# Two blocks of a sequence model in one launch: the order of VectorE's work in an attention step, and of one low part on GpSimd

## The reference

```
# 16 heads of 64, 4 key/value heads, blocks of 128 queries against 256 keys
s = einsum('bnqkgd,bnjkd->bnkgqj', qb, kk) * (HEAD_DIM ** -0.5)
s = where(mask, s, NEG_INF)
m = maximum(max(s, axis=-1), sink)
pr = exp(s - m)
w = pr / (sum(pr, axis=-1) + exp(sink - m))
o = einsum('bnkgqj,bnjkd->bnqkgd', w, vv)
h = h + o @ w_o
hm = h * rsqrt(mean(h * h) + eps) * norm_mlp      # rmsnorm, then the MLP
```

## Time and profile before

| | |
|---|---|
| time, median of 3 runs | 1812.46 us (1812.0 to 1815.38) |
| the profiled execution's own time | 1810.39 us |
| its span, first to last instruction | 1808.6 us |
| PE busy | 1744.2 us, 96% of the span |
| DVE, ACT, POOL busy | 898.0, 767.4 and 982.2 us |
| mean granted TensorE clock | 0.986 |
| attention loop | about 1243 to 1375 us |
| `wob` and the first two units of `up1` | about 1375 to 1412 us |

### The profile page before, as it was taken

One profiled execution on the slowest core, in us unless ns is written; L12 is line 12 of the kernel. 1 busy time (PEld: TensorE's weight loads), 2 busy tenths in 40 slices (PEclk: granted clock), 3 DMA queues, 4 the chain that ended last, 5 costly groups with the idle time before them and its releaser, 6 DMA issues.

```text
span 1808.6 us, 20962 instructions
## 1 busy us (share of the span) xinstructions
PE 1744.2 (96%) x8022; PEld 1424.6 (79%) x8022; DVE 898.0 (50%) x1298; ACT 767.4 (42%) x1205; POOL 982.2 (54%) x616
## 2 busy tenths in 40 slices
PE   9999999999997779999999999999999999999998
PEld 7887888777786777888888888887567788888886
DVE  3999987676674774532212122656655221212124
ACT  5333335377755573344223323533555331323234
POOL 5859555676555573654444445665436444444464
PEclk9999999999998999999999999999999999999999
DMA  4223223222221223223222223232102222322321
GB/s 166 98 90 100 100 92 125 86 88 81 100 79 49 65 84 132 97 94 101 93 96 103 93 95 103 83 105 70 36 24 70 93 93 96 102 94 94 104 93 59
DMA packets 54532, 164.05 MB, mean 91 GB/s; under 512 B 6304, under 2 KB 14112, under 8 KB 54304
## 3 DMA queue, kind: packets, MB, share of 16 engines
q1 hardware_dynamic: 54432, 162.71, 26.8%
HBM read 156.66 MB, written 6.03 MB: 90 GB/s over the span
## 4 chain that ended last, share of the span: by engine, by line
PE 65%; DVE 6%; ACT 5%; issue 4%; POOL 3%; DMA 0%; SPq 0%; POOLq 0%; DVEq 0%; ACTq 0%
PE B L313 52%; PE B L2226 1%; PE B L2137 1%; PE B L1634 1%; POOL ACC L366 1%; ACT WH L285 1%; PE B L296 1%; PE B L298 1%; PE B L297 1%; POOL WL L289 1%; PE B L1527 1%; DVE SW L1131 1%; PE B L2208 1%; PE B L1399 0%; PE B L2335 0%
## 5 line engine op out<-in xcount | busy, mean ns | idle before, releaser
L289 POOL TENSOR_TENSOR WL<-RAW,WH 128x1024 fp32r<-128x1024 f32 x281 | 682.5, 2431 | 623.6 <-ACT WH L285 623.5
L285 ACT ACTIVATE WH<-RAW 128x1024 fp32r<-128x1024 f32 x281 | 296.5, 1057 | 664.3 <-PE B L313 631.8
L313 PE MATMUL B<-P0h,WH 128*128 128x512 f32 x1104 | 434.1, 393 | 1.8 <-ACT WH L285 1.8
L313 PE MATMUL B<-P0l,WH 128*128 128x512 f32 x1104 | 426.4, 391 | 1.4 <-DVE P0l L430 1.3
L313 PE MATMUL B<-P0h,WL 128*128 128x512 f32 x1104 | 279.8, 391 | 1.9 <-POOL WL L289 1.9
L313 PEld LDWEIGHTS B<-P0h,WH 128*128 128x128 f32 x1104 | 208.4, 189 | 47.0 <-issue 2.9
L313 PEld LDWEIGHTS B<-P0l,WH 128*128 128x128 f32 x1104 | 208.3, 189 | 46.0 <-DVE P0l L430 2.3
L313 PEld LDWEIGHTS B<-P0h,WL 128*128 128x128 f32 x1104 | 207.9, 188 | 45.6 <-POOL WL L289 2.3
L437 DVE TENSOR_TENSOR H<-H,B 128x512 f32<-128x512 f32 x88 | 60.2, 685 | 281.1 <-PE B L313 281.1
L313 PE MATMUL B<-P1h,WH 128*128 128x512 f32 x448 | 174.7, 390 | 0.0
L1907 DVE SCALAR_TENSOR_TENSOR TMP<-B,RS 128x512 f32<-128x512 f32 x64 | 44.1, 691 | 260.1 <-PE B L313 244.0
(11 more groups left out here) (354 smaller groups left out, 2797.7 us busy)
## 6 DMA issues: line engine op xcount, KB each, us to landing
RAW<-in_w SPq DMA_DIRECT2D x281, 512.0 KB, 3.2
H<-in_xT SPq DMA_DIRECT2D x8, 256.0 KB, 5.1
g<-GB SPq DMA_DIRECT2D x8, 256.0 KB, 2.2
GB<-g SPq DMA_DIRECT2D x32, 64.0 KB, 2.0
out<-Q SPq DMA_DIRECT2D x4, 512.0 KB, 3.6
u<-TMP SPq DMA_DIRECT2D x7, 256.0 KB, 2.0
U<-u SPq DMA_DIRECT2D x28, 64.0 KB, 2.0
SPT<-in_ssm SPq DMA_DIRECT2D x1, 1040.0 KB, 5.7
```

The lines of the kernel that those rows point to most:

```text
L285: act.activation(WH[:, i % NS, :], RAW[:, i % NR, :], ACT.Copy).then_inc(*inc("w_hi", i))
L289: pool.tensor_tensor(WL[:, i % NS, :], RAW[:, i % NR, :], WH[:, i % NS, :].bitcast(F32), ALU.subtract).then_inc(*inc("w_lo", i))
L313: return pe.matmul(b[:, :], w[:, ws[c]], x[:, c, :], start=start, stop=stop)
```

## The change

DVE's list in a step of the attention loop is put in another order. Before: mask (n, 0), maximum (n, 0), sum and reciprocal of n-1, mask (n, 1), maximum (n, 1), the three small ones, then rope and `woa` work, then the low part of output n-2. After: sum and reciprocal of n-1, the low part of output n-3 (so the one that stood at the end of the step before), both masks, both maxima, the three small ones, then rope and `woa` work. The last output's low part follows behind the loop. On POOL, the low part of the weights that stood between the additions of squares 6 and 7 now stands behind that of square 7.

```
     def dve_scores(dve, n, hp):
         kv, blk, k0, nk, p_ = place(n)
-        st = AS[:, n, :]
         sv = s_view(n, hp)
...
         dve.scalar_tensor_tensor(sv, bv, 0.125, mv, ALU.mult, ALU.add).then_inc(*inc("att_s", ("s", n, hp)))
-        dve.wait_ge(*at("att_s", ("s", n, hp)))
-        dve.tensor_reduce(st[:, 2 * hp:2 * hp + 2], sv, AX.X, ALU.max).then_inc(*inc("att_d", (n, "max", hp)))
-        if hp == 0:
-            return
+
+    def dve_maxima(dve, n):
+        kv = place(n)[0]
+        st = AS[:, n, :]
+        for hp in range(2):
+            dve.wait_ge(*at("att_s", ("s", n, hp)))
+            dve.tensor_reduce(st[:, 2 * hp:2 * hp + 2], s_view(n, hp), AX.X, ALU.max).then_inc(
+                *inc("att_d", (n, "max", hp)))
         sk = sink[:, 4 * kv:4 * kv + 4]
...
         for n in range(18):
+            if 0 < n < 17:
+                dve_sum(dve, n - 1)
+            if n > 2:
+                dve_out(dve, n - 3)
             if n < 16:
                 dve_scores(dve, n, 0)
-            if 0 < n < 17:
-                dve_sum(dve, n - 1)
-            if n < 16:
                 dve_scores(dve, n, 1)
+                dve_maxima(dve, n)
...
-            if n > 1:
-                dve_out(dve, n - 2)
             if n == 2:
                 dve_p(dve, 1)
+        dve_out(dve, 15)
         dve_wo(dve, "woa", 7)
...
         for n in range(8):
             add_square(pool, "mlp1", n)
-            if n % 2 == 0:
+            if n in (0, 2, 4, 7):
                 lows(pool, IDX[("wob", 0, n // 2)] + 4)
```

## The result

The change takes 1803.74 us (median of 4 runs, 1802.59 to 1805.32) against 1812.23 us for the kernel before (4 runs, 1810.19 to 1815.38): a ratio of 0.9946, with a 95% interval of 0.993 to 0.9961. It is faster, by 8.5 us where 5.1 were forecast; the forecast time was 1807.4 us. A later series of the same pair gave 0.9956 (0.994 to 0.9971). The two profiled executions are 7.0 us apart, 1810.39 and 1803.37 us.

A forecast was written before the change was run, and what follows sets the result against it. PE is busy nearly all the time, its loop idle nearly all waits on DVE's mask; 2.05 us in the loop plus 3.05 behind it, 5.1 us, gives 1807.4 us from 1812.46. Bounds 1801.0 to 1818.4, range 1803.0 to 1811.2.

The forecast's parts named there:

- The squares: Behind the loop, POOL's edit: PE's 1.40 us wait for the last square and the 1.65 us low clock go, 3.05 us.
- The order, gain: In the attention loop, DVE's edit: second mask 1.0 us earlier against the first, 2.05 us gained in the loop.
- step 3's two waits turned into one: PE's first wait grows from 0.71 to about 1.6 us, the second of 0.89 goes, low clock kept: 0 gained.
- steps 6, 7 and 16 without a wait: PE's waits in these steps of the loop go: 0.3, 1.06 and 0.4 us gained.
- The order, price: POOL's low part starts earlier and can lie over DVE's small operations: 1.1 us held in step 3, some 1.5 in step 10.
- the small account of tenths: In steps 5 and 14 the last small operation just passes ahead of POOL's low part, by 0.1 us.
- one of the prediction's own signs of being wrong: In the profile after, L2167 or L2169 lasting over 2 us in steps 5, 7 or 14 would be wrong.
- the rule for two SBUF inputs: A two-SBUF-input VectorE instruction and a GpSimd one reading SBUF exclude each other; up to 2.3 us loss per low-part step.
- The first step: Step 11 of the loop: one wait of about 1.35 us in place of 1.67, 0.3 us gained, low clock kept.
- The rival that had this in it: More of the loop comes back, in step 11 or as low clocks: up to 3.3 us more, about 1804.2 us; 22%.
- The second: Base of the sum: profiled execution 2.07 us below the median, so 5.1 us is taken from the median, 1812.46.
- The slower rival: POOL's low part holds DVE in every loop step that has one: 5.7 us lost plus 3.3 low clock, 1818.4 us; 6%.

The follow-up runs named there:

- e1_square: The kernel before with only POOL's low part moved behind square 7, DVE's order kept; 1813.9 us, ratio 0.9977 to before.
- e3_maxima_between: The change with each maximum put back behind its own mask; 1808.94 us, ratio 0.9954 to before.
- e5_exp_waits_neg: The kernel before with the four exponentials waiting for the negated maxima alone, no longer for the last small operation; 1810.44 us, ratio 0.9966 to before.
- e2_order: The change with only DVE's new order, POOL's low part ahead of square 7 as before; 1805.91 us, ratio 0.994 to before.
- e6_low_halves: The change with each of the attention's low parts on POOL split into two instructions of 512 columns; 1801.72 us, ratio 0.9914 to before.
- e4_sum_behind_masks: The change with sum and reciprocal behind both masks, ahead of the maxima; 1814.25 us, ratio 0.9984 to before.

## Why the prediction was right and where it failed

**The squares** were right in every step: the order on GpSimd, the room on TensorE, the half clock that goes with the wait. 3.05 us forecast, 3.25 us in the tails of the two profiles; every kernel with this edit has a tail of 12.06 us, those without it 15.3.

**The order, gain.** Right: the masks 0.6 us apart, the first mask in its place, no wait left at the output product, step 3's two waits turned into one (1.56 us, I had 1.6), steps 6, 7 and 16 without a wait. In step 6 this was luck: the 0.3 us were to come because the hold of 2.29 us in step 5 was to go, and it stayed, at 2.27 us. Idle time in the loop was to fall by 2.05 us and fell by 4.99 - 3.11 = 1.88.

**The order, price.** That the low part would hold small operations was right, the small account of tenths was not, and one of the prediction's own signs of being wrong came up: a small operation of over 2 us in steps 5 and 7. Step 3 (1.29 us) and step 10 (1.65 us) were held as forecast. Step 5 was to pass by 0.1 us and was held for 2.27 us, which cost nothing more than before, since 2.29 us stood there already. Step 7 I had taken as free; the low part started 0.02 us ahead of the small operation and made the wait of 0.55 us in step 8. Step 14 passed. Step 11 came out at 1.00 us for 1.35. The errors nearly cancel: 0.55 us more in step 8, 0.35 less in step 11. And the 2.29 us with which the prediction says that the trace agrees with the rule for two SBUF inputs belong to L2169, which has one; L2170, which has two, shows it, with 2.40 to 2.45 us in e1_square.

**Two steps failed.** The forecast was 3.6 us too slow. Of these, 1.9 lie between the two profiled executions (7.0 us for 5.1), nearly all of it the 1.7 us of the first step below, and 1.7 in the way from profile to median, the second.

The first step is a term of the sum: "one wait of about 1.35 in place of 1.67: 0.3, low clock kept". The wait of 1.00 us in step 11 brought no half clock in any of the three profiles of this order, which is 1.7 us more. Why it doesn't stays open, for the length of the wait doesn't decide it: the two waits in step 11 of e3_maxima_between sum to 1.60 us and brought none, the two of before sum to 1.67 and brought one in all three profiles. The rival that had this in it named 1804.2 us and got 22%; of the 3.0 to 3.3 us that it adds, the profiles show these 1.7, so that the measured time lies so near its own is in part chance.

The second is the base of the sum: "it stands 2.07 below the median of the runs, so against the median I forecast". The distance was carried over from before to after without asking what it was, and it doesn't carry over: the profiled execution of the change lies 0.37 us below its median. Nor was "before, that low part mostly starts just behind the small operations" a fact of the kernel with one outcome. It is a race with a margin of 0.03 to 0.04 us, lost in a part of the executions; a lost one holds the chain for some 2.4 us and cost TensorE between nothing (steps 3 and 7 of e1_square) and 2.3 us of waits (step 10).

How much of the 8.5 us of the medians is the race's stays open. The two profiles account for 7.0 of them, and with four runs on each side the interval (7.1 to 12.7 us) begins there. For the race in the remaining 1.5 us speak e5_exp_waits_neg, which was to take only its price away and gains 6.0 us by the medians with a profile that gains 0.2, and e2_order, with 8.5 to 13.3 us by its ratio for 3.8 by a loop that is held against races won. Against it stands that the loop starts up to 4.2 us apart in executions of these kernels, for what happens ahead of it: the third profile of before won every race and took 1812.04 us, 0.4 below the median from which the forecast started, on another chip. In how many executions a race is lost can't be said from four profiles. The runs' scatter, present in all kernels, goes roughly with their mean clock (0.979 to 0.989 in the runs of before, but for one of 0.936 that took 1817.49 us), and what makes it stays open.

The slower rival, the low part over the small operations in every step that has one, happened in part (steps 3, 5, 7 and 10) and cost 0.55 us of wait in step 8 and, by the rows of step 10, probably the 1.00 us of step 11.

## What to carry to other kernels

When an instruction of one engine starts within a few hundredths of a microsecond of another's that it may not overlap, the trace shows one outcome of a race: profile the kernel twice more and look for operations of one line with two durations, before a sum is built on either. Put the short operations on the critical chain where no long instruction of the other engine can start, or cut the long one in two, which caps one hold (2.4 to 1.2 us here) but can hold two operations in a row, one by each half, as in step 10 of e6_low_halves. And in a loop in which several waits end at the same engine, look for what that engine does once and out of turn: the one moved split of step 2 was worth 3.4 us of the loop, nearly as much as the whole new order with 3.8 against a profile that had won its races. And where a median is forecast from one profile, set how far such profiles scatter beside the change that is forecast.

## What the hardware showed that I had not expected

- VectorE's 128x4 operation L2170 was held for 2.40 to 2.45 us in e1_square and in the second profile of before though it starts 0.03 us ahead of GpSimd's 128x1024 subtraction by the records, and passes in 0.15 us when it is 0.04 us ahead; but in step 7 of the first profile of before (1303.09 against 1303.12 us) and in the profile of e5_exp_waits_neg (1324.71 against 1324.74 us) it passes at 0.03. So the order in the records doesn't decide it to the last hundredth. The Trainium skill (page "SBUF — State Buffer", section "SBUF: two separate sides") says that of two such instructions the one that starts first gets the shared pair of ports for the whole instruction. The trace agrees but for these last hundredths: the held operation of step 10 in the second profile of before ends at 1330.24 us, the low part at 1330.22.
- The same wait of TensorE may or may not bring a half clock. Waits of 0.17 and 0.89 us in step 7, both with before's order, had no stretch at 0.50 behind them in the first and third profiles of before and had one in the second (and in that of e1_square); in step 3, 1.56 us brought one in both profiles of the change, and in e4_sum_behind_masks neither 1.30 us there nor 1.66 us in step 4 did.
